# A fused two-layer encoder step: two of each step's probability groups turned by fp32 products in column halves, and the root inverses taken one by one

## The reference

```
s = jnp.einsum('bqhd,bkhd->bhqk', q_c, k_c).astype(jnp.float32) * scale + bias
s = jnp.where(valid, s, NEG)
p = jax.nn.softmax(s, axis=-1).astype(v.dtype)
return jnp.einsum('bhqk,bkhd->bqhd', p, v_c)
```

## Time and profile before

| | us |
|---|---|
| median of 3 runs (2465.11 to 2466.1) | 2465.75 |
| profiled execution, its own time | 2466.24 |
| its span in the trace | 2464.4 |
| PE busy in the span | 2443.9 (99%) |
| DVE, ACT, POOL busy | 1541.8, 914.4, 238.5 |
| mean granted clock of TensorE, of full speed | 0.998 |

### The profile page before, as it was taken

One profiled execution on the slowest core, in us unless ns is written; L12 is line 12 of the kernel. 1 busy time (PEld: TensorE's weight loads), 2 busy tenths in 40 slices (PEclk: granted clock), 3 DMA queues, 4 the chain that ended last, 5 costly groups with the idle time before them and its releaser, 6 DMA issues. The chain is left out here.

```text
span 2464.4 us, 42981 instructions
## 1 busy us (share of the span) xinstructions
PE 2443.9 (99%) x16495; PEld 2392.6 (97%) x16495; DVE 1541.8 (63%) x2845; ACT 914.4 (37%) x1717; POOL 238.5 (10%) x545
## 2 busy tenths in 40 slices
PE   8999999999999999999999999999999999999998
PEld 7999999999999999999999999999999999999998
DVE  5666666677866666666666724427666666666666
ACT  6555555555433222222333641325222223322223
POOL 1111111113100000000000321221000000000000
PEclk9999999999999999999999999999999999999999
DMA  6122222454111110111111211112111111111012
GB/s 168 54 61 61 61 61 61 124 149 137 52 52 51 51 34 34 34 51 51 51 51 35 71 35 35 37 52 69 44 43 34 51 51 51 51 51 42 35 42 81
DMA packets 136522, 145.37 MB, mean 59 GB/s; under 512 B 4444, under 2 KB 125956, under 8 KB 136420
## 3 DMA queue, kind: packets, MB, share of 16 engines
q1 hardware_dynamic: 120420, 118.69, 15.2%
q0 software_dynamic: 14384, 23.03, 3.6%
q10 hardware_dynamic: 1616, 2.25, 0.3%
HBM read 125.97 MB, written 17.97 MB: 58 GB/s over the span
## 5 line engine op out<-in xcount | busy, mean ns | idle before, releaser
L167 PE MATMUL psum<-gx_hi,w_hi 128*128 128x352 f32 x3456 | 1123.7, 325 | 0.8 <-DVE gx_lo L229 0.4
L168 PE MATMUL psum<-gx_lo,w_hi 128*128 128x352 f32 x3456 | 1115.7, 323 | 0.0
L169 PE MATMUL psum<-gx_hi,w_lo 128*128 128x352 f32 x3456 | 1115.0, 323 | 0.0
L167 PEld LDWEIGHTS psum<-gx_hi,w_hi 128*128 128x128 f32 x3456 | 649.5, 188 | 3.3 <-issue 0.9
L168 PEld LDWEIGHTS psum<-gx_lo,w_hi 128*128 128x128 f32 x3456 | 649.7, 188 | 0.6
L169 PEld LDWEIGHTS psum<-gx_hi,w_lo 128*128 128x128 f32 x3456 | 649.5, 188 | 0.0
L1715 DVE TENSOR_TENSOR x<-x,psum 128x352 f32<-128x352 f32 x528 | 258.5, 518 | 119.1 <-PE psum L169 118.8
L1586 ACT ACTIVATE conv_t<-a_gate,cur 128x352 f32<-128x352 f32 x132 | 90.0, 682 | 539.5 <-DVE a_gate L1666 532.3
L168 PE MATMUL psum<-h_loB,w_hi 128*128 128x352 f32 x528 | 171.1, 324 | 0.0
L169 PE MATMUL psum<-h_hiB,w_lo 128*128 128x352 f32 x528 | 171.0, 324 | 0.0
L168 PE MATMUL psum<-h_loA,w_hi 128*128 128x352 f32 x528 | 170.9, 324 | 0.0
(11 more groups left out here) (197 smaller groups left out, 2965.5 us busy)
## 6 DMA issues: line engine op xcount, KB each, us to landing
raw<-in_f_w_up SPq DMA_DIRECT2D x44, 1024.0 KB, 5.1
raw<-in_f_w_down SPq DMA_DIRECT2D x22, 1024.0 KB, 4.9
raw<-in_a_w_o SPq DMA_DIRECT2D x25, 512.0 KB, 4.1
raw<-in_a_w_qkv SPq DMA_DIRECT2D x22, 512.0 KB, 3.8
raw<-in_b_w_in SPq DMA_DIRECT2D x8, 1024.0 KB, 5.7
raw<-in_b_w_out SPq DMA_DIRECT2D x4, 1024.0 KB, 5.2
gx_hi<-o_scratch POOLq DMA_DIRECT2D x3, 1232.0 KB, 7.7
gx_lo<-o_scratch POOLq DMA_DIRECT2D x3, 1232.0 KB, 10.8
```

The source lines that it names most:

```text
L167: pe.matmul(out, w[0], rhs[0], start=first, stop=False)
L168: pe.matmul(out, w[0], rhs[1], start=False, stop=False)
L169: return pe.matmul(out, w[1], rhs[0], start=False, stop=last)
```

## The change

`turn` keeps its place and its order. For groups 0 and 1 of the steps s = 0 to 7, each `pe.transpose` of 128 by 128 becomes two fp32 products with the identity as the moving operand: the first takes 64 key columns of the probabilities as weights and writes partitions 0 to 63, the second the other 64 and partitions 64 to 127. Group 2, and all of s = 8, stay transposes. `t_done` now rises by two for each group: once at the last product of each half, or by two at the last transpose; `copy` on ACT waits for twice the count. In `g_dve` the first set's three reciprocals are no longer made ahead of the first output but one ahead of each of the outputs 0, 1 and 2.

```
@@ turn
-                for j, kb in enumerate(key_groups(s)[i]):
+                group = key_groups(s)[i]
+                for j, kb in enumerate(group):
                     rows = key_rows(s, kb)
                     at = P * (kb - key_blocks(s)[0])
                     for h in range(2):
-                        mm = pe.transpose(psum[:rows, GROUP_BANK[i], P * (2 * j + h):P * (2 * j + h + 1)],
-                                          probs[g % 2][h][:, at:at + rows], ident[:, :])
-                mm.then_inc(t_done, 1)
+                        cut = slice(P * (2 * j + h), P * (2 * j + h + 1))
+                        if i < 2 and s < NB:
+
+                            for half in HEAD_ROWS:
+                                mm = pe.matmul(psum[half, GROUP_BANK[i], cut],
+                                               probs[g % 2][h][:, at + half.start:at + half.stop], ident[:, :],
+                                               start=True, stop=True)
+                                if kb == group[-1] and h == 1:
+                                    mm.then_inc(t_done, 1)
+                        else:
+                            mm = pe.transpose(psum[:rows, GROUP_BANK[i], cut], probs[g % 2][h][:, at:at + rows],
+                                              ident[:, :])
+                if not (i < 2 and s < NB):
+                    mm.then_inc(t_done, 2)
@@ copy (ACT)
-                act.wait_ge(t_done, turned_to(g) + i + 1)
+                act.wait_ge(t_done, 2 * (turned_to(g) + i + 1))
@@ v_set (DVE)
                 if first and o == 0:
                     g_split(None, dve, 1, 0)
-                    norm.dve_inverse(dve, range(NCH))
                 if first and o < NCH:
+                    norm.dve_inverse(dve, (o,))
                     norm.rstd_wait(dve, o)
```

## The result

| | before | after |
|---|---|---|
| median, us (6 runs each) | 2465.39 | 2515.15 (2514.66 to 2515.41) |
| ratio, 95% interval | | 1.0201 (1.0188 to 1.0214) |
| profiled execution, its time and span | 2466.24, 2464.4 | 2515.30, 2513.5 |

The change made the kernel 49.8 us slower, where +44.3 was predicted. The direction, the mechanism and the range hold. The sum is 5.5 us short, and that has a place of its own. The mean granted clock of TensorE is 0.999 of full speed beside 0.998 before, so the clock has no part in it.

A forecast was written before the change was run, and what follows sets the result against it. PE (TensorE), busy 99% of the span, was taken to bound the kernel. Products 44.9, layout +0.2, pB wait −0.4 and root inverses −0.4 gave +44.3 us: 2510 us, range 2497 to 2524.

The forecast's parts named there:

- The bound and the counts: In the attention PE's queue is set end to end; 416 transposes in `turn` become 1664 instructions, adding directly to the time.
- The price of a half product: In `turn`, 0.0545 us an instruction, 0.218 us a block in place of a transpose's 0.110: +44.9 us over 416.
- The floor of 0.027: Lower bound in us for one half-product instruction, taken from products with 32 moving columns.
- The changes of array layout: PE's loss of 0.21 us moves from before `turn` to before the projection: 0 over 64 steps, +0.2 at first turn.
- The other engines: ACT's copies behind `turn` move later by about 0.65 us; spare time stays or grows and no new wait comes.
- the wait for pB: `turn` waits 0.4 us for pB in the attention; this should go: −0.4 us.
- The root inverses: With one reciprocal ahead, PE's wait of 0.36 us for the first emptied bank goes: −0.4 us.
- The first, losses that don't cancel: Layout changes around `turn`: 13.4 us come off (2497 us, chance 0.05) or on top (2523 us, chance 0.07).
- The second, halves that don't run side by side: In `turn` an instruction costs 0.108 us, a block 0.432: +134 us, about 2600 us; chance 0.04.
- The third, issue as the bound at 128 columns: `turn` is bound by issue at 0.027 us an instruction, so the time stays at 2465 us; chance 0.03.

The follow-up runs named there:

- half_columns: The changed kernel with only 64 of the identity's 128 columns moving in the half products, so half of each turned block is left out: 2472.22 us.
- half_by_half: The changed kernel with all of a group's products of the lower half first, then all of the upper half: 2546.10 us.
- full_width: The changed kernel with one fp32 identity product over the full array for each of the 416 blocks, in place of two half products: 2515.20 us.
- turn_only: The kernel before with only the turning by half products added, the root inverses still three in a row: 2514.98 us.
- roots_only: The kernel before with only the root inverses taken one by one, the turning still by transposes: 2464.66 us.

## Why the prediction was right, and where its sum was short

- **The bound and the counts.** Right. Idle time hid nothing: 416 became 1664 instructions, and the span grew by what they take.
- **The price of a half product**, 0.0545 from `weigh` and the mixing: 0.0546 measured. With the transposes' 0.110 that is 416 × 0.1083 = 45.1 us, 0.2 off the term. `half_columns` shows that columns set it at 128 columns, and `half_by_half` that it holds only where a product finds a partner in the other half. The floor of 0.027 from the earlier trace rows was read a little low: the instructions start in pairs, and it is 0.03.
- **The changes of array layout: the term that was mis-sized.** "I set gain and loss equal: 0 over 64 steps", plus 0.2 once. The step starts of both traces, taken one by one, give +6.22 us for each pair of heads from the second to the seventh; 52 blocks × 0.1083 = 5.63 are products, and 0.59 remain, 4.7 us over 8 pairs. It has two parts. (a) In most steps 0.02 to 0.08, 0.055 in the mean: `weigh`'s own first products take some 0.05 longer than the next (437.20 − 436.06 is 1.14 us, where 20 × 0.0546 is 1.09), so the loss before a transpose is near 0.155 and not 0.21, while before L167 it is 439.31 − 0.16 − (438.73 + 0.218) = 0.20. I had put `weigh`'s entry into its exit. The earlier trace rows had given 0.25, and I noted the difference of 0.04 and dropped it. (b) In the step behind the sample's `weigh` 0.20: there the gain that I counted does not come. After, that step reads

```profile
399.88 0.42 PE L1064 MATMUL psum<-pT,vc 128*64 128x32 f32 x8
400.23 0.30 PE L1064 MATMUL psum<-pT,v 32*64 32x32 f32 x4
400.46 0.44 PE L1035 MATMUL psum<-ident,pA 128*64 128x128 f32 x4
```

  It is 0.23 us from the start of the sample's last four instructions, which use 32 rows, to halves that use 128, as much as to a transpose before (246.23 to 246.47 in that trace). Both have 64 weight columns; the rows differ. The moving columns differ too, 32 and 128, but not in the change just ahead, from the eight instructions of 128 rows to the four of 32: pairs of the eight start 0.06 us apart, and from the last pair, at 400.07, to the four it is 0.16. So a change of rows alone costs about 0.1 us there. In `full_width`, where that step has a change of layout at this place before and after, the step grows by 0.27 and not 0.42. I took "column halves" for one layout and had not looked at the rows of the shape.
- **The other engines.** Right: nothing new waits, and the wait for pB went. But it gave back some 0.2 us and not 0.4: its step grew by 0.27, where the same step of the other pairs grew by 0.49, because PE would have lost 0.15 to 0.2 of the 0.4 there to the change of layout anyway.
- **The root inverses.** The wait went in the profiled execution, but what it is worth hangs on when a load lands: 0.6 us from row sums to L167 in before's trace, nothing in `turn_only`'s, and not a fixed 0.4.
- **The rest.** 45.1 + 4.7 = 49.8; the first pair lacks 0.25 (most of it that wait for pB), the input stage ended 0.44 later in this profiled execution, and the wait for gm_t gave 0.6 back: 49.4 beside the spans' 49.1. The last 0.3 I leave open.
- **The rivals.** The first, losses that don't cancel, is what happened in part, at a third of its 13.4 us. The second, halves that don't run side by side though they share the moving identity, did not occur; `half_by_half` shows what brings it about, and it is the order and not the shared operand. Its cost, estimated by the Trainium skill's factor of 4 in "TensorE: Matmul & The Clock Gate", section "Terms", is not borne out: a full product measured 0.223 beside a transpose's 0.110, a factor of 2. The third, issue as the bound at 128 columns, fell with the 0.0546 of after and with `half_columns`, where as many instructions took 0.029 each.

`roots_only` has the lowest median of all versions; by the interval it is not told apart from before.

## What to carry to other kernels

Turn fp32 tiles by the transpose: a product with the identity costs twice as much on TensorE, in halves or over the full array. Where instructions of unlike array layout alternate, count the changes of layout in a step as well as the instructions, and count the rows of a shape as part of its layout; each change between column halves and the full array cost 0.15 to 0.2 us here, and one between 32 and 128 rows 0.1 or more. Half-width products ran side by side here only with products of the other half close by in the queue, two products across the border between runs of four, so alternate them.

## What was unexpected of the hardware

- The same 128 blocks of half products cost 15.1 us at the start of the turning and 35.1 at its end.
- Runs of four products of one half overlap with the other half's run by two products at either border, and the ones without a partner take 0.21 us and not 0.11.
- A change from 32 rows by 64 columns to 128 rows by 64 columns costs as much as one to the full array: 0.23 and 0.24 us from the start of the last four instructions of 32 rows.
- A product in halves with 32 moving columns costs no less than one with 64: 0.03 and 0.029 us an instruction, where 128 columns cost 0.0546.
- A full-array fp32 product with the identity takes 0.223 us where it repeats, and 0.32 directly behind a change of layout.
